# Two orders of work in a two-block transformer kernel: wide matmul units as eight and eight, and a state turn-back summed on TensorE

## The chip, the core and the metric

The kernel runs on one core of a Trainium2 chip, in one launch. The metric is the device time of that launch in microseconds (us). All data is float32; most matmuls read it in the `fp32r` form, and the large products are made from a rounded "high" part and a "low" remainder of both operands, so that one product is three matmuls (high by high, low by high, high by low).

## The reference

Two blocks follow each other on 256 tokens of width 2048. The first has an adaptive norm (its shifts and gains are `silu(c) @ ada_w`, a 2048 by 12288 product), a mixer of sparse attention (NSA) in four head groups and a gated linear recurrence (LRU), and a gated feed-forward part. The second has sliding-window attention and a state-space part (S5). Cut to what the change touches:

```python
# first block, one head group of the sparse attention: three branches, each a softmax
p_cmp = masked_softmax(q @ k_cmp); o_cmp = p_cmp @ v_cmp          # compressed keys
o_slc, o_win = softmax(q @ ks) @ vs, softmax(q @ kw) @ vw         # selected, windowed
o = gt0 * o_cmp + gt1 * o_slc + gt2 * o_win
# recurrence: h[t] = a[t] * h[t-1] + b[t]
# second block, state space: a complex state of 64 numbers for each of 64 groups
s[t] = (ab_re + i ab_im) * s[t-1] + b[t]
y = C_re @ s_re - C_im @ s_im + D_skip * u
```

## The kernel before

All large products form one long stream on TensorE. A *unit* is one 256-row slab of a weight matrix by 512 output columns; a group is 4 to 24 units that sum into one set of PSUM banks. For each unit SyncE loads the slab (`wraw`), ScalarE rounds it (`whi`, L1381), VectorE takes the remainder (`wlo`, L1386), and TensorE multiplies. ScalarE and VectorE run `LEAD` = 4 units ahead in their programs, over `HI` = 6 buffers. A plain unit is 24 matmuls of 256 moving columns (L1948). A *wide* unit (`gr.wide`) lays the high and low part of the activation side by side as 512 moving columns: for each of its two 128-row halves `kk` it issues four matmuls `whi` by 512 columns (L1938) and then four `wlo` by 256 columns (L1941). TensorE waits for `lo_ready` before the unit. The wide groups are most of the projections `pb`, `ga`, `gb`, `pa` and of the feed-forward part, 344 units in all.

Everything else is cut into *jobs*: Python generators whose pieces between two `yield`s are *steps*. `walk` runs every engine's program through the same units. After its own work of a unit an engine issues the steps that are due: a job with `steps` steps in the units `first` to `last` has issued `(u - first + 1) * steps // (last - first)` of them after unit `u`. Each engine's queue is strictly in this order, so a step that waits holds up all that follows on its engine. The `evac` jobs empty the banks of a group that is done. The places of the sparse attention (`nsa`, four head groups) and of the recurrence (`lru`, four parts), counted from the unit `a`, are written out by hand:

```python
for make, at in ((nsa, ((0, 16), (28, 43), (51, 66), (75, 88))), (lru, ((19, 28), (43, 51), (67, 75), (88, 96)))):
```

In `nsa` (26 steps for the first head group, 25 for the others) a step of VectorE scales the exponentials by their weights (L687 to L695), and the step behind it begins with TensorE's transposes of these (L724, L726), which wait for it. For the second to fourth head group these pairs are the steps (12, 13), (15, 16), (18, 19) and (21, 22). Step 4 makes the weights of the compressed branch (L638) and step 7 transposes them (L647).

`squares` makes sums for a norm: ScalarE squares four rows (L368), GpSimd adds them (L404, L406), and two steps later TensorE sums over the partitions (L376). It runs in the `evac` of `wout` and of the last `down`.

`states` runs the state space in 16 rounds `n`, beside `attention2` (four jobs, PE lines L932 to L1035), while TensorE is in the projections of the second block. In a round VectorE turns the inputs by tabulated phases (L1255 to L1258, into `wr`, `wi`), scans them (L1265, into `sx`, `sy`), and turns the states back: two products and a difference give `sr` (L1284 to L1287), two products and a sum give `si` (L1292 to L1295). In the round after it TensorE forms the outputs (`state_outputs`, L1220 and L1222, plain float32): for `q` = 0 and 1 one matmul of the real and one of the imaginary part, into 32 partitions each. VectorE then takes them from the bank (L1278). Each odd `n` a pair of ScalarE steps and the remainder `ys_lo` (L1318) follow.

## Time and profile before

| | |
|---|---|
| median of 3 runs | 2635.95 us (2635.82 to 2640.33) |
| the profiled execution, its own time | 2642.89 us |
| its span | 2640.8 us |
| mean granted TensorE clock | 0.988 |
| TensorE busy | 2572.3 us, 97% |
| VectorE busy | 1903.1 us, 72% |
| ScalarE busy | 1148.6 us, 43% |

"Busy" of an engine is time in which an instruction of it was under way. A matmul's recorded duration reaches past the start of the next, so what a matmul costs in a stream is the distance of the starts. The granted clock is 1.00 at full speed and 0.50 at half.

### The profile page before, as it was taken

How to read it: one execution, taken by the hardware profiler on the slowest of the kernel's cores; microseconds unless marked ns; L12 is line 12 of the kernel's file. 1: busy time of each engine (PE TensorE's matmuls, PEld its weight loads, DVE VectorE, ACT ScalarE, POOL GpSimd, SP SyncE). 2: the span in 40 equal slices, each digit the busy share in tenths (PEclk: the TensorE clock that was granted, in tenths of full speed). 3: DMA queues.
4: the chain of work that ended last, by engine and by line, in shares of the span. 5: the costliest groups of instructions: out<-in, count | busy, mean ns of one | idle time of the engine just before them, and what ended most of it. 6: DMA issues, size and time to landing. Idle time of an engine off the chain costs nothing.

```text
span 2640.8 us, 43075 instructions
## 1 busy us (share of the span) xinstructions
PE 2572.3 (97%) x17618; PEld 2360.0 (89%) x17618; DVE 1903.1 (72%) x2553; ACT 1148.6 (43%) x1426; POOL 223.3 (8%) x190
## 2 busy tenths in 40 slices
PE   7999999989999999999999999999999999999999
PEld 5799999989988899888888888899999888899999
DVE  7864777777777786678886686664467888887563
ACT  1033455555344443545443444444444445434432
POOL 0000000000000001000035662001000000000000
PEclk9998999999999999999999999999999999999999
DMA  9974556556888887577766777655465454465654
GB/s 403 426 267 137 182 169 217 175 176 222 281 283 280 278 285 271 150 236 235 236 226 229 218 222 217 190 184 181 148 211 178 146 150 150 150 191 174 200 195 133
DMA packets 243443, 567.81 MB, mean 215 GB/s; under 512 B 17424, under 2 KB 21520, under 8 KB 228784
## 3 DMA queue, kind: packets, MB, share of 16 engines
q1 hardware_dynamic: 233776, 530.33, 61.0%
q0 software_dynamic: 9472, 34.74, 3.8%
q8 instruction: 140, 2.29, 0.3%
q14 instruction: 55, 0.45, 0.1%
HBM read 550.85 MB, written 14.16 MB: 214 GB/s over the span
## 4 chain that ended last, share of the span: by engine, by line
PE 81%; DVE 8%; DVEq 3%; ACT 3%; DMA 2%; issue 2%; SPq 0%; POOLq 0%; ACTq 0%; POOL 0%
PE banks L1948 35%; PE banks L1938 24%; PE banks L1941 12%; DVE wlo L1386 3%; DMA wraw<-ada_wT_dram 2%; PE banks L1479 2%; ACT whi L1381 1%; DVEq L354 1%; PE banks L1953 1%; DVE wraw L1362 1%; PE banks L1928 1%; PE banks L562 1%; PE banks L785 1%; PE banks L1484 1%; PE banks L1206 0%
## 5 line engine op out<-in xcount | busy, mean ns | idle before, releaser
L1386 DVE TENSOR_TENSOR wlo<-wraw,whi 128x1024 fp32r<-128x1024 f32 x777 | 971.6, 1262 | 534.6 <-ACT whi L1381 507.3
L1381 ACT ACTIVATE whi<-wraw 128x1024 fp32r<-128x1024 f32 x777 | 814.2, 1057 | 1087.5 <-PE banks L1948 385.2
L1948 PE MATMUL banks<-h,whi 128*128 128x256 f32 x4032 | 754.0, 289 | 3.6 <-DVE h L473 1.8
L1948 PEld LDWEIGHTS banks<-h,whi 128*128 128x128 f32 x4032 | 637.2, 194 | 22.3 <-issue 17.5
L1948 PE MATMUL banks<-h,wlo 128*128 128x256 f32 x2016 | 574.5, 285 | 0.0
L1938 PE MATMUL banks<-h,whi 128*128 128x512 f32 x1920 | 526.8, 396 | 5.1 <-DVE h L477 3.2
L1948 PEld LDWEIGHTS banks<-h,wlo 128*128 128x128 f32 x2016 | 390.9, 194 | 0.0
L1938 PEld LDWEIGHTS banks<-h,whi 128*128 128x128 f32 x1920 | 329.4, 190 | 50.7 <-DVE h L477 4.3
L1941 PEld LDWEIGHTS banks<-h,wlo 128*128 128x128 f32 x1920 | 295.6, 189 | 41.1
L1941 PE MATMUL banks<-h,wlo 128*128 128x256 f32 x1920 | 306.3, 281 | 0.0
L1362 DVE SCALAR_TENSOR_TENSOR wraw<-wraw,cb 128x2048 f32<-128x2048 f32 x96 | 219.9, 2293 | 37.4 <-DMA wraw<-ada_wT_dram 36.2
L1948 PE MATMUL banks<-hid,whi 128*128 128x256 f32 x736 | 133.2, 284 | 0.0
L1948 PEld LDWEIGHTS banks<-hid,whi 128*128 128x128 f32 x736 | 114.7, 192 | 0.0
L1938 PE MATMUL banks<-hid,whi 128*128 128x512 f32 x384 | 104.8, 394 | 0.0
L1948 PE MATMUL banks<-hid,wlo 128*128 128x256 f32 x368 | 104.1, 283 | 0.0
L1479 PEld LDWEIGHTS banks<-h_f,wfour 128*128 128x128 f32 x384 | 74.2, 195 | 31.8 <-issue 20.7
L1479 PE MATMUL banks<-h_f,wfour 128*128 128x256 f32 x384 | 88.9, 389 | 11.8 <-DVEq L1465 11.8
L1948 PE MATMUL banks<-m,whi 128*128 128x256 f32 x480 | 88.2, 286 | 0.0
L1948 PEld LDWEIGHTS banks<-m,whi 128*128 128x128 f32 x480 | 76.1, 195 | 0.0
L1938 PEld LDWEIGHTS banks<-hid,whi 128*128 128x128 f32 x384 | 65.6, 189 | 8.8
L1948 PE MATMUL banks<-m_lo,whi 128*128 128x256 f32 x256 | 72.5, 283 | 0.0
L1948 PE MATMUL banks<-m_hi,whi 128*128 128x256 f32 x256 | 72.5, 283 | 0.0
(442 smaller groups left out, 3450.5 us busy)
## 6 DMA issues: line engine op xcount, KB each, us to landing
wraw<-w_in_dram SPq DMA_DIRECT2D x312, 512.0 KB, 3.7
wraw<-ada_wT_dram SPq DMA_DIRECT2D x96, 1024.0 KB, 5.7
wraw<-ffn_up_dram SPq DMA_DIRECT2D x192, 512.0 KB, 3.7
wraw<-ffn_down_dram SPq DMA_DIRECT2D x96, 512.0 KB, 3.6
wraw<-w_out_dram SPq DMA_DIRECT2D x64, 512.0 KB, 3.7
wfour<-w_in_dram SPq DMA_DIRECT2D x16, 1024.0 KB, 13.3
wraw<-proj_a_dram SPq DMA_DIRECT2D x32, 512.0 KB, 4.3
wraw<-proj_b_dram SPq DMA_DIRECT2D x32, 512.0 KB, 4.6
```

What stands on the lines that cost most here:

```text
L354: return ve.drain() if self.me == "dve" else None
L562: ins = te.matmul(bank[1][:, 0, 0:60], wcmp[which][:, l, :], blocks[:, l, :], start=(l == 0), stop=(l == 31))
L785: ins = te.matmul(bank[2 * a + n // 2][:, n % 2, :], wgate[:, a, n, :], t1[:, n, :], start=True, stop=True)
L1362: ve.scalar_tensor_tensor(out=row, in0=row, scalar=1.0, in1=cb[:, :], op0=ALU.mult, op1=ALU.mult, accum_out=mod[:, col:col + 1]).then_inc( ...
L1381: sc.activation(whi[:, r, 0:w], wraw[:, PLACE[z], 0:w], ACT.Copy).then_inc(hi_ready, 1)
L1386: ve.tensor_tensor(wlo[:, PLACE[z], 0:w], wraw[:, PLACE[z], 0:w], whi[:, r, 0:w].bitcast(F32), ALU.subtract).then_inc(lo_ready, 1)
L1479: ins = te.matmul(out, w[:, g * CB + o * P:g * CB + (o + 1) * P], x, start=(c == 0 and o % 2 == 0), stop=(c == DC - 1), skip_group_check=True)
L1484: ins = te.matmul(flat(bank[2 + b][:, :, :]), x[:, b * P:(b + 1) * P], w[:, 3 * CB:4 * CB], start=(c == 0), stop=(c == DC - 1))
L1928: ins = te.matmul(pair[:, 2 * b, 0:48], x[:, b * P:(b + 1) * P], w[:, k * 48:(k + 1) * 48], start=(k == 0 and t == 0), stop=(k == 15 and t ...
L1938: te.matmul(wides[g % 2][:, o, :, :], wh[:, cols(o)], X[gr.x][2][:, k, :, :], start=(k == 0), stop=(k == last), skip_group_check=True)
L1941: ins = te.matmul(wides[g % 2][:, o, 0, :], wl[:, cols(o)], hi[:, k, :], start=False, stop=(k == last), skip_group_check=True)
L1948: ins = te.matmul(out, w[:, at_w + o * P:at_w + (o + 1) * P], x, start=first, stop=(k == last and t == 2), skip_group_check=True)
```

## The change

Five edits. The wide unit becomes all eight `whi` matmuls of both halves and then all eight `wlo` matmuls; TensorE waits for `hi_ready` ahead of the first eight and for `lo_ready` ahead of the last eight. The turn-back of the states is no longer summed: VectorE writes four products `sr`, `si`, `sx`, `sy` (one of them negated), and TensorE sums them in four matmuls for each `q`. The scans work in place, with one new buffer `turning`, for which `atmp` moves. `squares` has one more step ahead of TensorE's sum where there is no gain. The units of `nsa` and `lru` shift: `nsa` has 17, 16, 16 and 14 units instead of 16, 15, 15 and 13, `lru` 8, 7, 7 and 8 instead of 9, 8, 8 and 8.

```diff
@@ squares
         yield
         yield
+        if scale is None:
+            yield
         j.take("pool_to_pe", "pe", added)
@@ state_outputs
-                te.matmul(bank[2][rows, 0, :], cz[:, m, 0, 2 * q2 + q, :], sr[:, q, :], start=True, stop=False,
-                          skip_group_check=True)
-                ins = te.matmul(bank[2][rows, 0, :], cz[:, m, 1, 2 * q2 + q, :], si[:, q, :], start=False, stop=True,
-                                skip_group_check=True)
+                for t, (part, x) in enumerate(((0, sr), (0, si), (1, sx), (1, sy))):
+                    ins = te.matmul(bank[2][rows, 0, :], cz[:, m, part, 2 * q2 + q, :], x[:, q, :], start=(t == 0),
+                                    stop=(t == 3), skip_group_check=True)
@@ states
-                        ve.tensor_tensor(a3(sx), er, states_in[:, :, a, :], ALU.mult)
-                        ve.tensor_tensor(a3(sy), ei, states_in[:, :, b, :], ALU.mult)
+                        ve.tensor_tensor(a3(o), er, states_in[:, :, a, :], ALU.mult)
+                        ve.tensor_tensor(a3(turning), ei, states_in[:, :, b, :], ALU.mult)
                         ve.drain()
-                        ve.tensor_tensor(a3(o), a3(sx), a3(sy), op)
+                        ve.tensor_tensor(a3(o), a3(o), a3(turning), op)
...
             if n < 16 and me == "dve":
-                ve.tensor_tensor(a3(wr), er, a3(sx), ALU.mult)
-                ve.tensor_tensor(a3(wi), ei, a3(sy), ALU.mult)
-                ve.drain()
-                ve.tensor_tensor(a3(sr), a3(wr), a3(wi), ALU.subtract)
-                ve.drain()
+                ve.tensor_tensor(a3(sr), er, a3(wr), ALU.mult)
+                ve.scalar_tensor_tensor(out=a3(si), in0=ei, scalar=-1.0, in1=a3(wi), op0=ALU.mult, op1=ALU.mult)
             yield
             if n < 16:
                 if me == "dve":
-                    ve.tensor_tensor(a3(wr), er, a3(sy), ALU.mult)
-                    ve.tensor_tensor(a3(wi), ei, a3(sx), ALU.mult)
-                    ve.drain()
-                    ve.tensor_tensor(a3(si), a3(wr), a3(wi), ALU.add)
+                    ve.tensor_tensor(a3(sx), er, a3(wi), ALU.mult)
+                    ve.tensor_tensor(a3(sy), ei, a3(wr), ALU.mult)
                 back = j.give("to_pe", "dve", j.drained())
@@ places of the jobs
-    for make, at in ((nsa, ((0, 16), (28, 43), (51, 66), (75, 88))), (lru, ((19, 28), (43, 51), (67, 75), (88, 96)))):
+    for make, at in ((nsa, ((0, 17), (27, 43), (50, 66), (74, 88))), (lru, ((19, 27), (43, 50), (67, 74), (88, 96)))):
@@ tensor, unit
-            pe.wait_ge(lo_ready, u + 1 - U4)
+            pe.wait_ge(hi_ready if gr.wide else lo_ready, u + 1 - U4)
...
+            if gr.wide:
+
+                tiles = [(2 * n + kk, o, slice(kk * CB + o * P, kk * CB + (o + 1) * P)) for kk in range(2) for o in range(4)]
+                for k, o, cols in tiles:
+                    if (k, o) == (1, 0) and gr.x in ("h2", "h3"):
+                        pe.wait_ge(S["to_pe"], j.ready[gr.x][0])
+                    te.matmul(wides[g % 2][:, o, :, :], wh[:, cols], X[gr.x][2][:, k, :, :], start=(k == 0), stop=(k == last),
+                              skip_group_check=True)
+                pe.wait_ge(lo_ready, u + 1 - U4)
+                for k, o, cols in tiles:
+                    ins = te.matmul(wides[g % 2][:, o, 0, :], wl[:, cols], hi[:, k, :], start=False, stop=(k == last),
+                                    skip_group_check=True)
```

TensorE's queue at the first round's outputs of the state space (`cz` holds the output factors; L1012 and L1014 before are L1015 and L1017 after, L1220 and L1222 are L1224), before and then after:

```order
L1948 MATMUL banks<-h_54,wlo 128x256
L1012 MATMUL banks<-ident,sm_118 128x128
L1014 MATMUL banks<-ident,sm_117 128x128 x2
L1220 MATMUL banks<-sr,cz 32x256
L1222 MATMUL banks<-si,cz 32x256
L1220 MATMUL banks<-sr,cz 32x256
L1222 MATMUL banks<-si,cz 32x256
L1948 MATMUL banks<-h_54,whi 128x256 x2
```

```order
L1948 MATMUL banks<-h_54,wlo 128x256
L1015 MATMUL banks<-ident,sm_118 128x128
L1017 MATMUL banks<-ident,sm_117 128x128 x2
L1224 MATMUL banks<-sr,cz 32x256
L1224 MATMUL banks<-si,cz 32x256
L1224 MATMUL banks<-sx,cz 32x256
L1224 MATMUL banks<-sy,cz 32x256
L1224 MATMUL banks<-sr,cz 32x256
L1224 MATMUL banks<-si,cz 32x256
L1224 MATMUL banks<-sx,cz 32x256
L1224 MATMUL banks<-sy,cz 32x256
```

Four matmuls stand there now for each `q` instead of two; nothing else moved between the units.

VectorE's queue in the turn-back of a round (wlo is L1386 before and L1383 after), before and then after:

```order
L1386 TENSOR_TENSOR wlo<-wraw,whi 128x1024 x3
L1284 TENSOR_TENSOR wr<-turns_94,sx 128x512
L1285 TENSOR_TENSOR wi<-turns_94,sy 128x512
L1287 TENSOR_TENSOR sr<-wr,wi 128x512
L1386 TENSOR_TENSOR wlo<-wraw,whi 128x1024
L1292 TENSOR_TENSOR wr<-turns_94,sy 128x512
L1293 TENSOR_TENSOR wi<-turns_94,sx 128x512
L1295 TENSOR_TENSOR si<-wr,wi 128x512
```

```order
L1383 TENSOR_TENSOR wlo<-wraw,whi 128x1024 x3
L1286 TENSOR_TENSOR sr<-turns_94,wr 128x512
L1287 SCALAR_TENSOR_TENSOR si<-turns_94,wi 128x512
L1383 TENSOR_TENSOR wlo<-wraw,whi 128x1024
L1291 TENSOR_TENSOR sx<-turns_94,wi 128x512
L1292 TENSOR_TENSOR sy<-turns_94,wr 128x512
```

Two sums of a round are gone from VectorE's queue.

VectorE's queue in the second head group of `nsa`, from the shifted scores (last line L676, after L679) to the first weights (L695, after L698); L1362 (after L1359) is one 2048-wide product of the adaptive norm. Before and then after:

```order
L676 TENSOR_SCALAR st<-st 128x4
L1386 TENSOR_TENSOR wlo<-wraw,whi 128x1024 x2
L1362 SCALAR_TENSOR_TENSOR wraw,mod<-wraw,cb 128x2048
L687 RECIPROCAL st<-st 128x4
L690 TENSOR_TENSOR st<-st,gates 128x4
L695 TENSOR_SCALAR sm_84<-sm_84,st 128x128 x2
L695 TENSOR_SCALAR sm<-sm,st 128x256 x2
```

```order
L679 TENSOR_SCALAR st<-st 128x4
L1383 TENSOR_TENSOR wlo<-wraw,whi 128x1024
L690 RECIPROCAL st<-st 128x4
L693 TENSOR_TENSOR st<-st,gates 128x4
L698 TENSOR_SCALAR sm_84<-sm_84,st 128x128 x2
L698 TENSOR_SCALAR sm<-sm,st 128x256 x2
L1383 TENSOR_TENSOR wlo<-wraw,whi 128x1024
L1359 SCALAR_TENSOR_TENSOR wraw,mod<-wraw,cb 128x2048
```

The weights moved ahead of one `wlo` and of the product L1362.

## Rows read from the trace of the kernel before

**Rows 1.** The page: TensorE's busy time, share and instructions

```profile
PE 2572.3 (97%) x17618; PEld 2360.0 (89%) x17618; DVE 1903.1 (72%) x2553; ACT 1148.6 (43%) x1426; POOL 223.3 (8%) x190
```

**Rows 2.** TensorE's waits, 262 to 620 us: total us, times, longest us

```profile
PE banks L724 <- DVE sm L695: 7.3, 5, 3.1
PE banks L647 <- DVE pc L638: 4.5, 1, 4.5
PE banks L752 <- DVEq L354: 2.2, 3, 1.1
PE banks L724 <- DVE smB L695: 1.3, 2, 0.7
```

**Rows 3.** Timeline of two engines in the second head group: start us, us

```profile
377.44 2.28 DVE L1362 SCALAR_TENSOR_TENSOR wraw<-wraw,cb 128x2048 f32<-128x2048 f32 x1
...
381.20 0.48 PE L724 MATMUL banks<-ident,sm 128*128 128x128 f32 x1 [3.12 <-DVE sm L695]
```

**Rows 4.** Stretches: us, then PE, PEld, DVE, ACT, POOL busy; PEclk; DMA

```profile
370.00:423.00 53.00, 48.78 (x354) 45.66 (x353) 38.26 (x79) 24.51 (x56) 0.00 (x0) 0.97 0.44 144
556.00:612.00 56.00, 51.61 (x355) 47.70 (x356) 41.19 (x87) 26.08 (x59) 0.96 (x2) 0.92 0.39 123
1011.00:1020.00 9.00, 8.63 (x59) 8.64 (x60) 7.05 (x6) 3.18 (x3) 0.26 (x1) 0.81 0.50 174
```

**Rows 5.** Timeline of TensorE: the first norm sum of wout

```profile
1011.37 0.61 PE L376 MATMUL banks<-ones,t 128*128 128x1 f32 x4 [1.50 <-POOLq L407]
```

**Rows 6.** Timeline of TensorE in a wide unit

```profile
1209.59 1.09 PE L1938 MATMUL banks<-h,whi 128*128 128x512 f32 x4
1210.52 0.64 PE L1941 MATMUL banks<-h,wlo 128*128 128x256 f32 x4
1211.00 1.09 PE L1938 MATMUL banks<-h,whi 128*128 128x512 f32 x4
```

**Rows 7.** The chain that ended last: eight plain units

```profile
329.64 23.03 PE banks L1948 x192
```

**Rows 8.** Timeline of TensorE at a round's outputs

```profile
2063.45 0.63 PE L1220 MATMUL banks<-sr,cz 128*32 128x256 f32 x4
2063.90 0.61 PE L1222 MATMUL banks<-si,cz 128*32 128x256 f32 x4
2064.44 0.50 PE L1948 MATMUL banks<-h,whi 128*128 128x256 f32 x2
```

**Rows 9.** Timeline of VectorE in the first half of a turn-back

```profile
2067.76 0.69 DVE L1284 TENSOR_TENSOR wr<-turns,sx 128x512 f32<-128x512 f32 x1
...
2069.13 0.69 DVE L1287 TENSOR_TENSOR sr<-wr,wi 128x512 f32<-128x512 f32 x1
2069.90 1.23 DVE L1386 TENSOR_TENSOR wlo<-wraw,whi 128x1024 fp32r<-128x1024 f32 x1
```

**Rows 10.** Stretches of the state space, columns as in rows 4

```profile
2034.00:2063.00 29.00, 27.10 (x211) 24.18 (x210) 24.61 (x53) 10.58 (x22) 0.53 (x1) 1.00 0.51 152
2063.00:2090.00 27.00, 26.77 (x203) 23.55 (x202) 21.64 (x38) 14.56 (x24) 1.08 (x2) 1.00 0.53 161
2090.00:2126.00 36.00, 31.95 (x236) 28.67 (x235) 32.63 (x68) 15.47 (x29) 0.53 (x1) 0.95 0.44 132
2126.00:2183.00 57.00, 56.82 (x451) 52.16 (x449) 48.34 (x78) 28.02 (x32) 1.60 (x3) 1.00 0.54 160
2183.00:2212.00 29.00, 27.09 (x210) 24.32 (x209) 24.79 (x50) 15.59 (x25) 1.07 (x2) 1.00 0.53 158
2212.00:2243.00 31.00, 29.41 (x225) 26.14 (x224) 25.25 (x49) 15.93 (x24) 0.53 (x1) 1.00 0.48 147
2243.00:2275.00 32.00, 27.97 (x215) 24.84 (x214) 27.77 (x56) 15.74 (x26) 1.07 (x2) 1.00 0.49 152
2275.00:2440.00 165.00, 165.00 (x1327) 154.43 (x1326) 140.07 (x184) 70.67 (x76) 3.19 (x6) 0.99 0.56 174
```

**Rows 11.** TensorE's waits, 1900 to 2500 us, columns as in rows 2

```profile
PE banks L1012 <- DVEq L354: 13.5, 8, 3.1
```

**Rows 12.** Timeline of VectorE: a `wlo` in the sixth round

```profile
2192.13 1.23 DVE L1386 TENSOR_TENSOR wlo<-wraw,whi 128x1024 fp32r<-128x1024 f32 x1 [0.68 <-ACT whi L1381]
```

More of the change, by code:

```diff
@@ L194, in build_program @@
     pt2 = put("pt2", rT + 4 * K, [P, 384])
-    atmp = put("atmp", rT + 5 * K + 512, [P, T])
+    turning = put("turning", rT + 6 * K, [P, 2, T])
     ph = put("ph", z1 + 16 * K, [P, 4, 32, 16])
@@ L231, in build_program @@
     bz = put("bz", off, [P, 2, 2, P])
+    atmp = put("atmp", off + 4 * K, [P, T])
     xg, yf = put("xg", off + 2 * K, [P, T]), put("yf", off + 3 * K, [P, T])
@@ L1263, in states @@
                         mg = MAG[:, 2 * n + q:2 * n + q + 1].broadcast_to([P, T])
-                        for o, i in ((sx, wr), (sy, wi)):
-                            ve.tensor_tensor_scan(out=o[:, q, :], data0=mg, data1=i[:, q, :], initial=0.0, op0=ALU.mult,
+                        for o in (wr, wi):
+                            ve.tensor_tensor_scan(out=o[:, q, :], data0=mg, data1=o[:, q, :], initial=0.0, op0=ALU.mult,
                                                   op1=ALU.add)
@@ L1929, in unit @@
                                             start=(k == 0 and t == 0), stop=(k == 15 and t == 2))
-            for kk in range(0 if gr.mode == "GATES" else 2):
+            if gr.wide:
[9 more added lines that the diff above has]
+                                    skip_group_check=True)
+            for kk in range(0 if gr.mode == "GATES" or gr.wide else 2):
                 k, at_w = 2 * n + kk, kk * CB
@@ L1933, in unit @@
                     pe.wait_ge(S["to_pe"], j.ready[gr.x][0])
-                if gr.wide:
-                    cols = lambda o: slice(at_w + o * P, at_w + (o + 1) * P)
-                    for o in range(4):
-                        te.matmul(wides[g % 2][:, o, :, :], wh[:, cols(o)], X[gr.x][2][:, k, :, :], start=(k == 0),
-                                  stop=(k == last), skip_group_check=True)
-                    for o in range(4):
-                        ins = te.matmul(wides[g % 2][:, o, 0, :], wl[:, cols(o)], hi[:, k, :], start=False, stop=(k == last),
-                                        skip_group_check=True)
-                elif "T" in gr.mode:
+                if "T" in gr.mode:
                     for o in range(4 if gr.mode == "T" else 2):
```

## The prediction, made before the changed kernel was run

> **What bounds the kernel now.** The page first: TensorE is busy for 2572.3 us of the span of 2640.8 [rows 1]. The time is the length of its queue plus the places where it stands still or runs at half clock. So an edit is worth what it adds to or takes from TensorE's queue, plus what it does to those few waits. The view of TensorE's waits shows two fields of them that the change touches. One is the sparse attention, 262 to 620 us, where TensorE waits for VectorE 15.3 us in all [rows 2]. The other is the second block's attention beside the state space, 13.5 us in front of the transposes L1012 [rows 11]. The stretches show the clock there: a mean of 0.97 over 53 us and 0.92 over 56 us in the sparse attention [rows 4], 0.95 over 36 us in the state space [rows 10]. Each such mean is some stretches at half clock (1.2 GHz instead of 2.4) that began at or after a wait, and costs its shortfall times its length: 1.6, 4.5 and 1.8 us. In the wide stretches I read single units.
>
> **Wide units.** A half of a wide unit takes 0.93 us for its four 512-column matmuls and 0.48 us for its four of 256, start to start [rows 6]: 1.41 us, or 2.81 for a unit. The same 16 matmuls in another order are 1.86 and 0.95 us, again 2.81. Do the changes of kind (512 to 256 and back) cost something, of which two in four would be saved? A plain unit has none of them, streams the same 6144 columns, and takes 23.03 / 8 = 2.88 us [rows 7]. So no row shows a cost of a change of kind, and I reckon no gain. The other bound comes from the same row: its 256-column matmuls stand 23.03 / 192 = 0.120 us apart, eight in a row would take 0.96 instead of 0.95, and 344 units would cost 3.4 us more. I take 0, nearest to the rows of wide units themselves. The later wait for `wlo` gains nothing either, since TensorE does not wait there: in none of the views does a wide unit wait for `wlo`, and where TensorE stands still behind the norm ahead of the feed-forward part it waits for rows of `h`, which the first eight matmuls need as well. What covers this edit is that VectorE is some two units ahead; without that cover it would save up to 0.95 us a unit.
>
> **The sum over partitions one step later.** TensorE waits 1.50 us for GpSimd in front of L376 [rows 5], and the 9 us behind it have a mean clock of 0.81, which is 1.7 us [rows 4]. One step later is a unit of 2.88 us later, more than 1.50, so the wait and what follows it go: 3.2 us less. The same step in the last `down` stands before no wait, and costs nothing.
>
> **The places of nsa and lru.** The steps of a job fall on units by whole numbers. Twenty-five steps in 15 units give the running count 1, 3, 5, 6, 8, 10, 11, 13, ..., so the steps 12 and 13, the weights of VectorE and the transposes of TensorE that wait for them, stand in the same unit. In 16 units the count is 1, 3, 4, 6, 7, 9, 10, 12, 14, 15, 17, 18, 20, 21, 23, 25, and none of the four pairs shares a unit. The trace shows what the shared unit costs: in the second head group VectorE has a 2.28 us product L1362 in front of the weights, and TensorE waits 3.12 us [rows 3]. The queue of the changed kernel has the weights ahead of that product and of one `wlo`. So this wait goes, and with it the 1.6 us of clock. The other waits for weights and for `scores_used` are 7.3 - 3.1 + 2.2 + 1.3 = 7.7 us [rows 2]; some of them stand in places that the new counts leave alone (the pair 21, 22 of two head groups is where it was), so I take half, 3.8 us. The largest wait, 4.5 us at L647, is another thing: VectorE comes late out of the recurrence. There both the work and the transposes move one unit earlier, and one `wlo` between a product L1362 and the recurrence's products falls away. Estimate: 1.5 us less, with the 4.5 us of clock behind it kept. Against that, the last head group (13 to 14 units) gets the pair (15, 16) into one unit where it had (12, 13), behind a convolution of VectorE: 1 us more. The sum: 3.1 + 1.6 + 3.8 + 1.5 - 1.0 = 9.0 us less. Its bounds: nothing, if the shorter `lru` gives as much back, and all of the waits with their clock, 15.3 + 1.6 + 4.5 = 21.4 us.
>
> **The turn-back.** TensorE first. In a round the four records of L1220 start 0.45 us ahead of those of L1222, and the whole takes 0.99 us to the next unit's matmul [rows 8]. Each float32 matmul is two records. The records of one line stand together although the queue alternates between the lines (the rows of the queue above), so the matmuls of `q` = 0 and `q` = 1, which write different strips of 32 partitions, run at the same time. Two more matmuls for each `q` are then two more such groups, 0.90 us a round and 14.4 us in 16 rounds. VectorE saves two sums of 0.69 us and the drains ahead of them. Three operations with their drain take 2.14 us up to the next `wlo` [rows 9]; two take the 1.37 us to L1287's start or a little less. That is 0.77 us for each half, 1.55 a round. The negated product is a `scalar_tensor_tensor` of the same size, and in-place scans are the same scans, so I reckon both at nothing.
>
> What VectorE's time is worth is decided round by round, from the length less the busy time of each stretch [rows 10]. Where TensorE waits, the end of the stretch is set by VectorE's run of work; I follow that run back to what began it.
> - 2034 to 2063, 1.90 us waited: VectorE's run begins behind the outputs themselves, so it comes 0.90 later and is 1.55 shorter: -0.65.
> - 2063 to 2090, 0.23 waited: 0.90 - 0.23 = +0.67.
> - 2090 to 2126, 4.05 waited: VectorE's run began ahead of the outputs, -1.55; the waits left are 4.05 - 0.90 - 1.55 = 1.6, and I let the clock recover, -1.8.
> - 2126 to 2183, two rounds, 0.18 waited: 1.80 - 0.18 = +1.62.
> - 2183 to 2212, 1.91 waited: VectorE itself waits 0.68 us for ScalarE behind the turn-back [rows 12], so its saved time goes into that wait: +0.90.
> - 2212 to 2243, 1.59 waited: 0.90 - 1.59 = -0.69.
> - 2243 to 2275, 4.03 waited: -1.55.
> - 2275 to 2440, eight rounds, TensorE busy throughout: +7.20.
>
> Together +5.95, and with the clock +4.1 us.
>
> A rule of the Trainium skill speaks against the pairs. Its page "TensorE: Matmul & The Clock Gate", section "The mechanism", says that only weight loads are pulled ahead, and that matmuls start and end strictly in program order. By that rule the two strips could overlap at one place only, where `q` changes, and the edit would add eight single slots of 0.22 us, 1.76 us a round instead of 0.90; the sum would be 13.8 us higher, 2641.7 us. It is the mild form of rival 2. The trace disagrees: all four records of L1220 start before those of L1222 [rows 8].
>
> **Sum.** 0 - 3.2 - 9.0 + 4.1 = -8.1 us. The profiled execution, 2642.89 us, becomes 2634.8. It stood 6.9 us above the median of the runs, which becomes 2635.95 - 8.1 = 2627.9 us.
>
> **Rivals.**
> 1. *The shift of nsa and lru gives nothing.* The recurrence, squeezed by a unit, makes VectorE as late for the attention as it was. For it: VectorE's longest lateness (4.5 us) comes right out of the recurrence. Against it: the counts, and the queue, in which the weights are ahead. The sum is then -3.2 + 4.1 = +0.9, or 2636.9 us; with wide units at 0.96 for their eight small matmuls as well, 2640. Chance 0.24.
> 2. *The two strips fall out of step.* With four matmuls, eight records, of `q` = 0 queued ahead of the first of `q` = 1, TensorE may not look far enough. A record's slot is 0.45 / 2 = 0.22 us; 16 in single file are 3.6 us instead of 0.99, or +2.6 a round and 41.6 for 16. The waits of the first eight rounds take up at most their 13.9 us. The outcome ends on the slow side: 2635.95 - 3.2 - 9.0 + 41.6 - 13.9 = 2651.5 us, and up to 2665 if nothing is taken up. It decides from (3.2 + 9.0 + 13.9) / 16 = 1.6 us a round on, which is where the rest of the change is used up. For it: no row shows more than four records of a strip ahead of the other strip. Against it: four are no obstacle now. Chance 0.13.
> 3. *More waits go than I count.* If nearly all of the waits in the sparse attention vanish with their clock, 21.4 instead of 9.0 us, the time is 2615.5 us. Against it: three of the pairs stay where they were. Chance 0.13.
>
> **How the numbers follow.** Forecast 0.50, with 2622 to 2633 as its own range; rival 1 0.24, rival 2 0.13, rival 3 0.13. The range 2615 to 2645 holds the forecast, rival 1 with the dearer wide units, most of rival 3 and a half of rival 2's smallest outcomes. A difference of 0.2% is 5.3 us, about what a measurement of this kernel can tell from none. Faster by more than that (below 2630.7) are rival 3 and most of the forecast: 0.55. Within it: the rest of the forecast and most of rival 1, 0.26. Slower: rival 2 and a little of rival 1, 0.19.
>
> **What would show it.** Wide units at 2.81 us, start to start, and no wait for `wlo` (the wide step). No wait at L376 near 1011 us and full clock behind it. No wait for weights of 3 us in the second head group, a wait of about 3 us at L647. In the state space 16 records of outputs in 1.9 us, in four groups of four, and waits before the transposes that sum to some 4 to 7 us instead of 13.5. The prediction is wrong if the outputs take near 3.6 us a round, if wide units change by more than 0.01 us each, or if new waits of VectorE stand behind the recurrence.

## The result, and the profile after

The changed kernel takes 2659.57 us (median of 3 runs, 2658.97 to 2663.11) against 2635.95 before: a ratio of 1.0076, 95% interval 1.0062 to 1.0089. It is slower by 0.8%, and outside the predicted range. The profiled execution has a span of 2661.3 us, 20.5 more than before.

The page's first part, as [rows 1]:

```profile
PE 2594.6 (97%) x17746; PEld 2375.4 (89%) x17746; DVE 1878.3 (71%) x2521; ACT 1148.9 (43%) x1426; POOL 224.8 (8%) x190
```

VectorE has 32 instructions fewer and is 24.8 us less busy, as meant. TensorE has 128 matmul records more and is 22.3 us busier; the prediction had priced these records at 14.4 us.

Where the time went is seen by the end of each unit in both traces. The table gives the start of the unit's last matmul, after less before; the units' numbers run through the whole stream (the last two units of `wout` and of the second `down`, which are issued by rows, are left out of the count, so that behind them a number is two and then four below the kernel's own).

| unit (us before) | 60 (258) | 100 (421) | 120 (498) | 140 (582) | 160 (657) | 280 (995) | 300 (1057) | 540 (1750) | 620 (2011) | 660 (2169) | 700 (2324) | 740 (2451) | last |
|---|---|---|---|---|---|---|---|---|---|---|---|---|---|
| after less before, us | -0.3 | +1.1 | +1.3 | +14.0 | +8.8 | +7.4 | +4.2 | +1.1 | -0.8 | +2.9 | +10.0 | +20.5 | +20.5 |

So the last head group of the sparse attention cost some 8 us (units 120 to 160; 9.1 us from unit 60 on), the sum over partitions gave 3.2 back (280 to 300), the wide units shed 13.4 ns each, 4.6 us in 344, and the state space cost 21.3 us. The 1.9 us that went between 540 and 620 are not explained here. (With the code unchanged, profiles differ by up to 4 us at unit 60, and by steps of 1.5 us behind waits, each a stretch at half clock that comes or stays out. Differences below that size are read here from many units or not at all.)

TensorE's waits in the sparse attention, as [rows 2] (L727 was L724, L650 was L647, L755 was L752), and then in the state space, as [rows 11]:

```profile
PE banks L727 <- DVE smB L698: 8.5, 3, 5.8
PE banks L650 <- DVE pc L641: 8.1, 2, 6.6
PE banks L755 <- DVEq L355: 3.8, 5, 2.0
PE banks L662 <- DVEq L355: 2.0, 1, 2.0
```

```profile
PE banks L1015 <- DVEq L355: 6.1, 4, 2.3
```

The 7.3 us behind `sm` went; the forecast had counted on their greater part. But the wait for `pc` grew from 4.5 to 6.6 us, and a new one of 5.8 us for `smB` stands there: 20.4 us in the lines that answer to the 15.3 of [rows 2]. In the state space 7.4 us of waits went, so the 21.3 us come from what TensorE does.

TensorE at one round's outputs, as [rows 8], one execution of L1224's 16 records:

```profile
2185.93 0.62 PE L1224 MATMUL banks<-sr,cz 128*32 128x256 f32 x2
2186.39 0.59 PE L1224 MATMUL banks<-si,cz 128*32 128x256 f32 x2
2186.82 0.38 PE L1224 MATMUL banks<-sx,cz 128*32 128x256 f32 x1
2186.82 0.40 PE L1224 MATMUL banks<-sr,cz 128*32 128x256 f32 x1
2187.03 0.38 PE L1224 MATMUL banks<-sx,cz 128*32 128x256 f32 x1
2187.07 0.38 PE L1224 MATMUL banks<-sr,cz 128*32 128x256 f32 x1
2187.25 0.38 PE L1224 MATMUL banks<-sy,cz 128*32 128x256 f32 x1
2187.28 0.38 PE L1224 MATMUL banks<-si,cz 128*32 128x256 f32 x1
2187.47 0.38 PE L1224 MATMUL banks<-sy,cz 128*32 128x256 f32 x1
2187.50 0.38 PE L1224 MATMUL banks<-si,cz 128*32 128x256 f32 x1
2187.71 0.59 PE L1224 MATMUL banks<-sx,cz 128*32 128x256 f32 x2
2188.14 0.59 PE L1224 MATMUL banks<-sy,cz 128*32 128x256 f32 x2
2188.67 0.51 PE L1948 MATMUL banks<-h,whi 128*128 128x256 f32 x2
```

This view is the centre of the case. A *slot* is the 0.216 us from the start of one record, or of two that run at the same time, to the start of the next. The first `sr` of `q` = 1 starts at 2186.82, when four records (`sr`, `si`) of `q` = 0 have run alone and four are left, and `q` = 1's `sx` and `sy` then run alone. That is 4 + 4 + 4 = 12 slots of 0.216 us, and 2.74 us to the next unit's matmul instead of 0.99: 1.75 us a round more, 28.0 in 16. (Three of the 16 rounds ran in part at half clock, with a granted clock of 0.90, 0.67 and 0.63, and took 3.04, 3.94 and 4.28 us; before, one did, with 0.50 and 1.86 us. All 16 together are 30.1 us longer, and with the 7.4 us of waits taken off, that is near the 21.3.) Note also that `sr` of `q` = 1 starts before `sy` of `q` = 0, which stands ahead of it in the queue.

### The profile page after: what moved, and what is told of

Same layout as the page of the kernel before. It is cut to its first block, busy times and chain, and to the rows that moved or that the text cites. A ratio compares the mean times of both kernels' runs of the same rounds, so it can differ in the third digit from the quotient of the medians.

```text
span 2661.3 us, 43251 instructions
## 1 busy us (share of the span) xinstructions
PE 2594.6 (97%) x17746; PEld 2375.4 (89%) x17746; DVE 1878.3 (71%) x2521; ACT 1148.9 (43%) x1426; POOL 224.8 (8%) x190
## 4 chain that ended last, share of the span: by engine, by line
PE 83%; DVE 8%; DVEq 3%; ACT 3%; DMA 2%; issue 1%; SPq 0%; ACTq 0%
PE banks L1948 36%; PE banks L1933 23%; PE banks L1937 12%; DVE wlo L1383 3%; DMA wraw<-ada_wT_dram 2%; PE banks L1476 2%; PE banks L1224 2%; ACT whi L1378 1%; DVEq L355 1%; DVE wraw L1359 1%; PE banks L1953 1%; PE banks L1925 1%; PE banks L565 1%; PE banks L788 1%; PE banks L1481 1%
## 5 line engine op out<-in xcount | busy, mean ns | idle before, releaser
L1383 DVE TENSOR_TENSOR wlo<-wraw,whi 128x1024 fp32r<-128x1024 f32 x777 | 972.9, 1263 | 557.6 <-ACT whi L1378 533.8
L1378 ACT ACTIVATE whi<-wraw 128x1024 fp32r<-128x1024 f32 x777 | 813.7, 1057 | 1085.4 <-PE banks L1948 406.6
L1948 PEld LDWEIGHTS banks<-h,whi 128*128 128x128 f32 x4032 | 637.1, 194 | 22.4 <-issue 17.4
L1948 PE MATMUL banks<-h,wlo 128*128 128x256 f32 x2016 | 574.2, 285 | 0.0
L1933 PE MATMUL banks<-h,whi 128*128 128x512 f32 x1920 | 483.2, 394 | 5.7 <-DVE h L480 3.9
L1933 PEld LDWEIGHTS banks<-h,whi 128*128 128x128 f32 x1920 | 346.2, 189 | 69.1 <-DVE h L480 4.9
L1948 PEld LDWEIGHTS banks<-h,wlo 128*128 128x128 f32 x2016 | 391.0, 194 | 0.0
L1937 PEld LDWEIGHTS banks<-h,wlo 128*128 128x128 f32 x1920 | 262.7, 191 | 18.8
L1937 PE MATMUL banks<-h,wlo 128*128 128x256 f32 x1920 | 268.3, 283 | 0.0
L1359 DVE SCALAR_TENSOR_TENSOR wraw<-wraw,cb 128x2048 f32<-128x2048 f32 x96 | 219.9, 2293 | 31.8 <-DMA wraw<-ada_wT_dram 30.8
L1933 PE MATMUL banks<-hid,whi 128*128 128x512 f32 x384 | 96.2, 392 | 0.0
```

What stands on the lines that cost most here:

```text
L1359: ve.scalar_tensor_tensor(out=row, in0=row, scalar=1.0, in1=cb[:, :], op0=ALU.mult, op1=ALU.mult, accum_out=mod[:, col:col + 1]).then_inc( ...
L1378: sc.activation(whi[:, r, 0:w], wraw[:, PLACE[z], 0:w], ACT.Copy).then_inc(hi_ready, 1)
L1383: ve.tensor_tensor(wlo[:, PLACE[z], 0:w], wraw[:, PLACE[z], 0:w], whi[:, r, 0:w].bitcast(F32), ALU.subtract).then_inc(lo_ready, 1)
L1933: te.matmul(wides[g % 2][:, o, :, :], wh[:, cols], X[gr.x][2][:, k, :, :], start=(k == 0), stop=(k == last), skip_group_check=True)
L1937: ins = te.matmul(wides[g % 2][:, o, 0, :], wl[:, cols], hi[:, k, :], start=False, stop=(k == last), skip_group_check=True)
L1948: ins = te.matmul(out, w[:, at_w + o * P:at_w + (o + 1) * P], x, start=first, stop=(k == last and t == 2), skip_group_check=True)
```

## The experiments

Each ratio is to the kernel before, run on the same chip beside it. In the diffs the base is named first.

### One part at a time

**e1_states_only**: of the change only `states`, `state_outputs` and the buffers.

> The kernel before with the edit of the states alone (four products, four matmuls for each strip). Theory A, the edits add up by place: between the units 620 and 740 the changed kernel fell back from -0.8 to +20.5 us, so this kernel takes 2636 + 21 = 2657 us, with eight slots of 0.216 us more in each of the 16 rounds. Rival, the places of the jobs or the wide units push VectorE late there: then this kernel alone stays at 2640 to 2645.

Measured: ratio 1.0071 (1.0056 to 1.0086). The units 620 to 740 take 21.2 us more, as in the changed kernel. So this part alone makes the kernel slow.

**e2_outputs_by_turns**: the changed kernel with the two loops exchanged.

```diff
-            for q in range(2):
...
-                for t, (part, x) in enumerate(((0, sr), (0, si), (1, sx), (1, sy))):
+            for t, (part, x) in enumerate(((0, sr), (0, si), (1, sx), (1, sy))):
+                for q in range(2):
...
```

> The changed kernel with the eight output matmuls of a round in another order: for each of the four terms first the strip of q = 0, then that of q = 1. Theory A, TensorE finds the other strip's matmul only a few records ahead: all 16 records now run in pairs, 8 slots instead of 12, no row starts alone; 4 slots of 0.216 us less in each round are 13.8 us less on TensorE; some of it comes back as waits for VectorE, so 2646 to 2650 us. Rival, the extra matmuls cost what they cost in any order: no change, 2659 us.

Measured: 1.0022 (1.0013 to 1.0032), 2646.87 us. The order alone gives back 15 of the 21 us: 740 stands 6.4 us above 620. These 6.4 us are what the turn-back still costs in this order: a round takes 1.85 us instead of 0.99, 13.7 us in 16, and the waits before the transposes fell by 6.5 us only, from 13.5 to 7.0. All 16 records go in pairs, in 8 slots:

```profile
2182.51 0.63 PE L1224 MATMUL banks<-sr,cz 128*32 128x256 f32 x4
2182.96 0.60 PE L1224 MATMUL banks<-si,cz 128*32 128x256 f32 x4
2183.40 0.60 PE L1224 MATMUL banks<-sx,cz 128*32 128x256 f32 x4
2183.83 0.60 PE L1224 MATMUL banks<-sy,cz 128*32 128x256 f32 x4
```

**e3_places_only**: the kernel before with the changed line of places.

> The kernel before with only the new places of nsa and lru. Theory A: the fall-back of 9 us that the changed kernel had by unit 160 is of this edit alone, 2645 us, with waits of some 6 us at the compressed branch's transposes and behind the convolution in the last head group. Rival: the clock's half-speed stretches at other places made it, then near 2636 us.

Measured: 1.0037 (1.0023 to 1.0051). The places lose by themselves: 6.9 us from unit 100 to 160, with the same waits as in the changed kernel (6.6 us at L647, 5.8 at L724).

**e4_wide_only**: the kernel before with the changed wide unit.

> The kernel before with only the wide units as eight and eight. Theory A: a wide unit takes 2.793 us instead of 2.807, 344 of them 4.6 us less, 2631 us. Rival: that gain is from some other edit, then 2636 us.

Measured: 0.9977 (0.9967 to 0.9987), 0.27 us less for each 20 wide units, 4.6 in all.

### How far TensorE looks across the strips

**e7_three_terms**: the changed kernel with three products in the sum; it leaves out `sy`, so its outputs lack that term.

```diff
-                for t, (part, x) in enumerate(((0, sr), (0, si), (1, sx), (1, sy))):
+                for t, (part, x) in enumerate(((0, sr), (0, si), (1, sx))):
...
```

> The changed kernel without the fourth product of the outputs (sy times its factor is left out of the sum, so the outputs lack that term; VectorE still makes it), still all of q = 0 and then all of q = 1. Theory A (TensorE starts a matmul of the other strip only when no more than four records of the strip in hand stand ahead of it): q = 0 has 6 records, of which the first 2 go alone, then 4 pairs, then the last 2 of q = 1 alone: 8 slots of 0.216 us, 1.73 us a round against 12 slots, 2.60 us, of the changed kernel; 16 x 0.86 = 13.8 us less, of which the waits ahead of the transposes take some back, so 2645 to 2650 us. Theory B (as soon as a strip has more than two matmuls the strips do not overlap at all but for the change of q): 6 + 6 - 2 = 10 slots or more, 2.2 us a round, 2652 to 2656 us. Theory C (the cost has to do with the number of matmuls alone, a slot and a half each): 9 slots.

Measured: 1.0024 (1.0015 to 1.0034), units 620 to 740 +6.5 us. Two records go alone, then come four pairs, then two go alone:

```profile
2181.94 0.62 PE L1224 MATMUL banks<-sr,cz 128*32 128x256 f32 x2
2182.39 0.38 PE L1224 MATMUL banks<-si,cz 128*32 128x256 f32 x1
2182.40 0.40 PE L1224 MATMUL banks<-sr,cz 128*32 128x256 f32 x1
...
2183.04 0.38 PE L1224 MATMUL banks<-sx,cz 128*32 128x256 f32 x1
2183.07 0.38 PE L1224 MATMUL banks<-si,cz 128*32 128x256 f32 x1
2183.28 0.59 PE L1224 MATMUL banks<-sx,cz 128*32 128x256 f32 x2
```

Those are theory A's 8 slots; 9 or 10 fit neither the view nor the time.

**e11_outputs_halves**: the changed kernel, two and two by turns.

```diff
-            for q in range(2):
...
-                for t, (part, x) in enumerate(((0, sr), (0, si), (1, sx), (1, sy))):
+            four = ((0, sr), (0, si), (1, sx), (1, sy))
+            for q, t in ((0, 0), (0, 1), (1, 0), (1, 1), (0, 2), (0, 3), (1, 2), (1, 3)):
+                for part, x in (four[t],):
...
```

> The changed kernel with the outputs in the order q = 0: sr, si; q = 1: sr, si; q = 0: sx, sy; q = 1: sx, sy. Theory A (a strip may run ahead of the other by four records, and no more): each group of four records finds its partner, all 16 records go in pairs, 8 slots, 1.73 us, as with q by turns, 13 to 15 us less than the changed kernel. Rival (the strips must take turns matmul by matmul, or each change back to q = 0 waits for q = 1 to end): 12 slots or more, 2.6 us or more a round, and the time of the changed kernel.

Measured: 1.0026 (1.0014 to 1.0038), units 620 to 740 +8.2 us against 21.3. Four records of one strip ahead of the other cost nothing; the 16 go in pairs, in 8 slots, here in the round at 2351 us:

```profile
2350.82 0.63 PE L1225 MATMUL banks<-sr,cz 128*32 128x256 f32 x4
2351.27 0.61 PE L1225 MATMUL banks<-si,cz 128*32 128x256 f32 x4
2351.71 0.62 PE L1225 MATMUL banks<-sx,cz 128*32 128x256 f32 x4
2352.14 0.62 PE L1225 MATMUL banks<-sy,cz 128*32 128x256 f32 x4
2352.69 0.50 PE L1949 MATMUL banks<-h,whi 128*128 128x256 f32 x2
```

### The places, taken apart

All four start from the kernel before and differ in one line:

```diff
 e5 +  (nsa, ((0, 17), (27, 43), (50, 66), (75, 88))), (lru, ((19, 27), (43, 50), (67, 75), (88, 96)))
 e6 +  (nsa, ((0, 17), (27, 43), (50, 66), (75, 88))), (lru, ((19, 27), (43, 50), (67, 74), (88, 96)))
 e9 +  (nsa, ((0, 17), (27, 43), (50, 66), (74, 87))), (lru, ((19, 27), (43, 50), (67, 74), (88, 96)))
 e14 + (nsa, ((0, 16), (28, 43), (51, 66), (76, 89))), (lru, ((19, 28), (43, 51), (67, 75), (88, 96)))
```

**e5_places_last_back**

> The kernel before with the shifted places of nsa and lru, but the last head group and the third part of the recurrence where they were (75 to 88, 67 to 75). Theory A (the loss of the places sits in the last head group alone, where the pair of steps 15 and 16 falls into one unit behind a convolution, and where the head group starts a unit earlier while VectorE comes no earlier out of the recurrence): the wait at L724 near 588 us of 6 us and the 6.7 us at L647 become about 3 and 4.5 us, unit 160 stands at +0 to +1 instead of +6.7, and the time is 2633 to 2638 us, the same as before or just below. Theory B (the shorter lru parts one and two make VectorE late from 262 us on): most of the loss stays, 2643 us or more.

**e6_places_lru_short**

> As the run with the last head group put back, but the third part of the recurrence stays one unit shorter (67 to 74), while the last head group starts at 75. It tells the two edits at 556 us apart. Theory A (VectorE's queue from the recurrence through to the first products of the head group sets the end; ending the recurrence's steps a unit earlier only moves work of the same length): the wait at L647 is 4.5 us or up to 2 us less, since the recurrence's products stand one wlo earlier, and the time is 2631 to 2638 us. Theory B (the squeezed recurrence itself makes VectorE late): the wait at L647 is 6 us or more, and the time 2638 us or more.

**e9_places_last_13**

> The kernel before with the shifted places of nsa and lru, but the last head group in 13 units from 74 (74 to 87) instead of 14 (74 to 88): the pair of steps 15 and 16 no longer shares a unit, the pair (12, 13) does as before, and the head group still starts one unit early. Theory A (the 6 us wait at L724 near 588 us is the pair (15, 16) behind the convolution; the 6.7 us at L647 is the early start): the 6 us wait falls to 2 or 3 us, L647 stays at 6 to 7 us, unit 160 stands at +1 to +4 instead of +6.7, and the time is 3 to 6 us below that of the shifted places. Theory B (an early start alone makes VectorE late for all of the head group): both waits stay, and the time is that of the shifted places, about 2649 us in its own job.

**e14_last_later**

> The kernel before with the last head group one unit later, in the same 13 units (76 to 89 instead of 75 to 88), nothing else changed. The wait at L647 is 6.6 us with the start at 74 and 4.5 us with the start at 75. Theory A (VectorE comes out of the recurrence at its own time, whatever the place of the transposes; each unit later takes some 2.1 to 2.9 us off the wait): 1.6 to 2.4 us at L647, and the time 2 to 5 us below before. Rival (VectorE's steps for the head group move too, and the wait moves with them): 4 us or more stay, and the time is that of before.

Measured, with the two waits of the last head group:

| last head group | ratio (95%) | wait at L647 | longest at L724 | units 100 to 160 |
|---|---|---|---|---|
| 75 to 88, before | 1 | 4.5 us | 1.9 us | 0 |
| 74 to 88, e3 | 1.0037 (1.0023 to 1.0051) | 6.6 | 5.8 | +6.9 |
| 74 to 87, e9 | 1.0028 (1.0015 to 1.0042) | 6.6 | 1.3 | +3.8 |
| 75 to 88, lru 67 to 75, e5 | 1.0007 (0.9997 to 1.0018) | 4.5 | 1.9 | -0.1 |
| 75 to 88, lru 67 to 74, e6 | 1.0009 (0.9999 to 1.0018) | 4.8 | 1.9 | +0.2 |
| 76 to 89, e14 | 1.0002 (0.9991 to 1.0013) | 2.8 | 6.0 | -0.3 |

The start of the head group sets the wait at L647, 2 us for each unit, and the length of the recurrence's part does not (e6 against e5): that is theory A of e5 and e9. It is that of e14 in kind only: the wait was 2.8 us where 1.6 to 2.4 had been expected, and the gain of 2 to 5 us did not come. The 6 us at L724 comes and goes with another thing. It is there in e3 and in e14, where the steps of a pair, (15, 16) in the one and (12, 13) in the other, both fall on the unit `a` + 82 with the convolution; it isn't in e9, where they don't. Nor is it in the kernel before, where the pair (12, 13) shares the unit `a` + 81, one ahead of the convolution. By run times e9 can't be told from e3, since their intervals overlap; the difference is one of the traces. VectorE there in the changed kernel:

```profile
582.70 1.22 DVE L1383 TENSOR_TENSOR wlo<-wraw,whi 128x1024 fp32r<-128x1024 f32 x1 [2.88 <-ACT whi L1378]
583.84 5.09 DVE L882 SCALAR_TENSOR_TENSOR t<-banks,vec,t 128x255 f32<-128x255 f32 x12
588.85 0.17 DVE L690 RECIPROCAL st<-st 128x4 f32<-128x4 f32 x1
589.09 0.16 DVE L693 TENSOR_TENSOR st<-st,gates 128x4 f32<-128x4 f32 x1
589.33 0.48 DVE L698 TENSOR_SCALAR sm0B<-sm0B,st 128x128 f32<-128x128 f32 x2
589.73 0.61 DVE L698 TENSOR_SCALAR smB<-smB,st 128x256 f32<-128x256 f32 x2
```

and TensorE behind it:

```profile
590.39 0.47 PE L727 MATMUL banks<-ident,sm0B 128*128 128x128 f32 x1 [5.80 <-DVE smB L698]
```

The convolution L882 takes 5.09 us, and the wait is 5.8. In e14 what the first wait lost the second one took, so the time is that of before. The three head groups ahead of it (e5) moved the waits among themselves: those for `sm` are 2.8 us instead of 7.3, but those at L647, L752, L724 for `smB` and L659 are 16.3 instead of 8.7.

### Wide units

**e8_wide_squares**: the two edits that gained, alone.

> The two edits that gained by themselves and nothing else: wide units as eight and eight, and the step ahead of TensorE's sum over the partitions. The wide units gave 4.6 us and the step 3.2 us in the changed kernel; if they add up, 7.8 us less than before, a ratio of 0.997 and about 2628 us (0.9955 to 0.9985). Rival: the earlier units move the other jobs' waits, as in the state space, and give back up to 3 us.

Measured: 0.9968 (0.9954 to 0.9982), 2631.47 us. In its trace they add up: the wide units are 4.6 us shorter and units 280 to 300 3.3 us. The run times alone don't tell it from e4, whose interval it overlaps.

**e10_wide_twos**: the kernel before, two `whi` and two `wlo` by turns.

```diff
+                for two in (tiles[0:2], tiles[2:4], tiles[4:6], tiles[6:8]):
+                    for k, o, cols in two:
...
+                        te.matmul(wides[g % 2][:, o, :, :], wh[:, cols], X[gr.x][2][:, k, :, :], start=(k == 0), stop=(k == last),
+                                  skip_group_check=True)
+                    for k, o, cols in two:
+                        ins = te.matmul(wides[g % 2][:, o, 0, :], wl[:, cols], hi[:, k, :], start=False, stop=(k == last),
+                                        skip_group_check=True)
```

> The kernel before with wide units as two whi matmuls and two wlo matmuls by turns, four times: eight changes of kind in a unit instead of four (before) or two (the changed kernel). Theory A (each change of kind costs about 13.4 / 2 = 6.7 ns, so that eight and eight saved two of them a unit): a unit takes 2.807 + 0.027 = 2.833 us, 344 units 9.2 us more than before, ratio about 1.0035. Theory B (what was saved belongs to the fifth to eighth 512-column matmul in a row, which start 226.7 ns apart, and runs of two cost what the first two of a run of four do, 233 and 236 ns, and 117 and 119 ns): 4 x (233.3 + 235.8 + 117.5 + 119.2) = 2.823 us, 5.7 us more. Theory C (it is the wait for lo_ready ahead of a unit that cost the time): 2.807 us and no change.

Measured: 0.9968 (0.9956 to 0.998), 2.787 us a unit. All three theories fell: eight changes of kind are cheaper than four.

**e12_wide_snake**: e8 with the parts of every second unit exchanged.

```diff
+                for part in ((0, 1) if n % 2 == 0 else (1, 0)):
+                    if part == 1:
+                        pe.wait_ge(lo_ready, u + 1 - U4)
...
```

> The wide and the squares edit alone, and besides every second unit of a wide group does its eight wlo matmuls first and then its eight whi, so that whi and wlo run sixteen in a row across two units: one change of kind a unit instead of two. Theory A (a change costs 6.7 ns): 2.3 us less than with the two edits alone, 2.786 us a wide unit. Theory B (the gain belongs to the fifth whi matmul in a row on, 226.7 instead of 232.5 ns, while wlo goes to 120.0 instead of about 117): the first four whi of every second unit gain some 23 ns, its first wlo lose some 6 ns, so 8 ns a unit, 2.9 us less. Rival C (the wait for wlo at the head of every second unit and the later end of the last reader of whi show): 2.80 us a unit or more, and new waits of VectorE.

Measured: 0.9956 (0.9942 to 0.997), 2628.32 us, the lowest ratio of all, though its interval overlaps those of e8 and e10. Mean of a wide unit 2.783 us:

```profile
1498.56 3.82 PE L1942 MATMUL banks<-h,whi 128*128 128x512 f32 x16
1502.22 2.08 PE L1945 MATMUL banks<-h,wlo 128*128 128x256 f32 x16
1504.13 1.09 PE L1942 MATMUL banks<-h,whi 128*128 128x512 f32 x4
```

The 16 `whi` take 3.66 us and the 16 `wlo` 1.91. In the trace the `whi` behind a run of `wlo` start 233, 236, 228, 233 and 231 ns apart and from the sixth on 226.7; the `wlo` 113, 119 and then 120.0. A long run of each is 8 x 226.7 + 8 x 120.0 = 2773 ns a unit. This is theory B's mechanism, with 10 ns a unit gained over e8 where it gave 8.

**e13_wide_ones_squares**: the squares edit, and one `whi` and one `wlo` by turns.

> The squares edit, and wide units as one whi and one wlo matmul by turns, eight times. Measured so far, over the 2773.3 ns of eight whi at 226.7 and eight wlo at 120.0 ns: 20 ns for each run of eight wlo, 16.7 ns for each run of four, 3.3 ns for each run of two. Theory D (a whi matmul starts its successor late only when several wlo matmuls stood in a row ahead of it; a single one costs nothing): 2773 ns a unit, 33 ns less than before, 11.5 us in 344 units, and with the 3.2 us of the squares edit a ratio of about 0.9944. Theory E (a change costs at least what it does in runs of two): 8 x 3.3 ns over the base, 2800 ns, 2.3 us less than before, 5.5 us with the squares edit, ratio 0.998.

Measured: 0.9967 (0.9953 to 0.998). Theory D held in the feed-forward part (units 320 to 540, 2773 ns each), and failed in the first block's projections, where each such unit takes 2827 ns, 20 more than before. The order has more than one steady pace: at the faster one the `whi` and `wlo` start their successors after 230.0 and 116.7 ns, at the slower one after 236 and 117, with the granted clock at 1.00 in both.

**e15_ones_squares_later**: e13 with the last head group at 76 to 89.

> The squares edit, wide units by ones, and the last head group one unit later. If the three gains add up (11.5, 3.2 and 2 to 5 us by the theories of the other two runs) it is the fastest: 17 to 20 us below before, ratio 0.993. If the last head group gives nothing, it is equal to the run without that edit.

Measured: 0.9992 (0.9977 to 1.0007). The later head group gave nothing here either, and the whole was not the fastest. Its trace stands 6.2 us above e13's at the end, 5.5 of it in steps of up to 1.6 us between the units 600 and 660, where the two programs are the same; these are stretches at half clock. The granted clock is 0.97, 0.97 and 0.90 in e15 from 1900 to 1950, 2050 to 2100 and 2100 to 2150 us, against 1.00, 1.00 and 0.97 in e13, which makes 6.5 us more of shortfall (each mean's shortfall times its 50 us). Why they came in one trace and not in the other is open.

**e16_snake_and_ones**: one by one in `gate` and `val` of the feed-forward part, 192 units, and e12's order in the other 152. The expectation counts all 240 units of the feed-forward part as one by one, but the edit asks for `gr.x == "h2"`, which leaves the 48 wide units of `down` out.

> The squares edit; the wide units of the feed-forward part (240) as one whi and one wlo by turns, the other 104 wide units with whi and wlo sixteen in a row across two units. If the start distances measured in each place add up: 240 x 33.3 ns + 104 x 23.3 ns = 10.4 us, with the 3.2 us of the squares edit 13.6 us less than before, ratio 0.9948, against 11.2 us (0.9956 measured) for sixteen in a row in all. Rival: the slower pace of the one by one order (2.827 us) comes with whatever stands ahead of it, and shows in the feed-forward part now; then 0.9965 or more.

Measured: 0.9969 (0.9956 to 0.9981). The rival held. The `gate` and `val` units of the first half take 2773 ns, the `down` units 2783 on average, and from unit 447 on, where the one by one order comes back right behind e12's, `gate` and `val` take 2827. In e13 the same units stayed at 2773. What the three traces with this order (e13, e15, e16) have in common is the entry. The faster pace began behind the stops ahead of the feed-forward part, where most units took 3 to 5 us; the slower one began where the order followed other matmuls without a stop, plain units in e13 and e15, sixteens in e16. How that sets the pace is open, and one by one is no order to rely on.

## Why the prediction was wrong

Its own steps, in order:

- **Wide units**, reckoned at 0: mis-sized. Each is 13.4 ns shorter, 4.6 us. The prediction read the unit as 2.81 us to two decimals and compared it with a plain unit, which has other matmuls in it. The gain isn't that of a change of kind saved either, since eight changes cost less than four (e10). The rows place it: behind a run of 256-column matmuls five of 512 columns start their successors late, by 27.5 ns in all, and the first two of 256 columns behind a run of 512 start theirs early, by 7.5 ns. In runs of two (e10) the lateness never runs its length and the early ones come each time: the `wlo` stand 116, 113, 113 and 119 ns apart instead of 120.0. The prediction's own sign of being wrong, a change of more than 0.01 us in a wide unit, was passed. The price over 2773 ns is 20 ns a unit for runs of eight, 33 for runs of four, 13 for runs of two, 10 for runs of sixteen.
- **The sum over partitions**, -3.2 us: right in number, and in part by luck. The wait at L376 is gone from the trace and units 280 to 300 took 3.2 us less. But the 1.7 us of clock are a feature of that one trace. In nine traces without this edit TensorE waits 0.5 to 2.3 us at L376, and from 1005 to 1030 us the clock is 0.93 in four of them (before, e5, e6, e9) and 1.00 in five (e1, e3, e4, e10, e14). In e4 it waited 1.48 us there, at 1006.74, and the clock from 1008 to 1017 us was 1.00.
- **The places**, -9.0 us: the step that failed in sign, by 17 to 18 us: 7.5 us more between units 120 and 160, 9.1 from unit 60 on. Its first part held: the wait of 3.12 us in the second head group is gone. Two parts fell. "Both the work and the transposes move one unit earlier" was to save 1.5 us at L647; VectorE did not come earlier, TensorE did, and the wait grew by 2.1 us. And the pair (15, 16) in one unit "behind a convolution: 1 us more" was 5.8: the convolution is 5.09 us long, which could have been read from the trace before (eleven of its twelve products are one row of 4.70 us there), and VectorE had first waited 2.88 us for ScalarE. Rival 1 saw no gain there; none saw a loss, though "new waits of VectorE" stand among the signs of being wrong.
- **The turn-back**, +4.1 us: mis-sized by 17 us, and here it is one sentence, "the matmuls of `q` = 0 and `q` = 1 run at the same time. Two more matmuls for each are two more such groups". With 0.90 us a round more TensorE would have had 8 slots; it had 12, because the other strip was reached only when four records were left. The rest of the step held: with the order that keeps 8 slots (e2) the list of stretches, +5.95 us without its clock term, came to +6.4, and at 2283 us to +0.5 against -1.25 listed. The 1.8 us for a recovering clock did not come in e2.
- **Rival 2**, chance 0.13, was what happened in the outputs, in its mild form: 1.75 us a round against the 1.76 given. "For it: no row shows more than four records of a strip ahead of the other strip" was the true reading, and deserved more than 0.13, since an extrapolation from four to eight carried the largest term of the sum.

The page "TensorE: Matmul & The Clock Gate" of the Trainium skill, section "The mechanism", says that matmuls start in program order. Its price was right here, but its reason isn't what the trace shows: `sr` of `q` = 1 starts at 2186.82, `sy` of `q` = 0 at 2187.25, and e7 and e11 show overlap that the rule excludes. What the runs bear out is a look ahead over four matmul records of another strip: 4 ahead, all in pairs (before, e11); 6 ahead, two alone (e7); 8 ahead, four alone (after). Whether it is counted in records or in something that grows with them, such as the weight loads between, is open.

## What to carry to other kernels

Matmuls that write different 32-partition strips overlap, but issue them by turns, or at most two float32 matmuls of one strip at a time; four in a row made 12 slots out of 8 and cost TensorE 28 us for the 25 us that VectorE saved. Even by turns the edit lost 6.4 us here (e2): work taken off an engine that is not the bottleneck is worth only the waits that go with it. Before a schedule is shifted by a unit, list for each wait what the waiting engine and the late engine do in that unit: a shift moves the earlier one alone, and one shared unit with a 5 us job behind it undoes several small gains. Where a loop runs hundreds of times, read its unit to the nanosecond over many repeats: 13 ns in 2807 were 4.6 us. And a half-clock stretch read in one trace is no term to count on before a second trace shows it.

## What was not expected of the hardware

- Start distances of 128-row matmuls with new weights each, at full clock, settle at 226.7 ns for 512 columns and 120.0 ns for 256. After a run of 256-column ones the next five of 512 are slower by 27.5 ns in all; after a run of 512-column ones the first two of 256 are faster by 7.5 ns.
- The same 16 matmuls one by one had two steady paces in one program, at full clock: 2773 and 2827 ns.
- Eight plain float32 matmuls for two strips take 8 or 12 slots of 0.216 us by their order alone.
